# Writing a weight slab's low part over the raw slab, and loading the slot again after its last use

## The reference

```python
# first_block
proj = rmsnorm(x, g) @ w_in                       # 7 column groups per head, and two gates
o_a  = gated_delta_rule_chunked(q, k, v, g, beta) # 8 heads
o_b  = forgetting_attention(fq, fk, fv, log_f)    # 8 heads
merged = sigmoid(gate_a) * (o_a @ w_proj_gdn) + sigmoid(gate_b) * (o_b @ w_proj_fox)
h = x + merged @ w_out
x = h + square(relu(rmsnorm(h, g2) @ w_up)) @ w_down
# second_block
rq, rk, rv, rg, aq, ak, av, gate_a, gate_b = split(rms_norm(x, g) @ w_in_2 + b_in_2)
# retention on 4 heads, windowed attention on 16, each projected, gated and merged
x = x + merged @ w_out_2
x = x + (silu(h2 @ w_ffn_gate) * (h2 @ w_ffn_up)) @ w_ffn_down
return rms_norm(x, g3)
```

## Time and profile before

| | us |
|---|---|
| median of 3 executions (1887.64 to 1888.70) | 1888.69 |
| the profiled execution's own time | 1888.82 |
| its span, first to last instruction | 1887.0 |
| PE (matmul) busy | 1876.8, 99% of the span |
| GpSimd (POOL) busy | 1091.8, 58% |
| VectorE (DVE) busy | 1252.6, 66% |
| ScalarE (ACT) busy | 777.7, 41% |
| 16 DMA engines, slab queue | 27.9% of their time |

### The profile page before, as it was taken

How to read it: one execution, slowest core, us unless ns; L and a number is a source line. 1 busy time by engine, 2 the same in 40 slices (tenths; PEclk the granted TensorE clock), 3 DMA queues, 4 the chain that set the end, 5 groups by cost and what they waited for, 6 DMA issues and landing times.

```text
span 1887.0 us, 31991 instructions
## 1 busy us (share of the span) xinstructions
PE 1876.8 (99%) x11773; PEld 1606.0 (85%) x11773; DVE 1252.6 (66%) x2128; ACT 777.7 (41%) x1526; POOL 1091.8 (58%) x1221
## 2 busy tenths in 40 slices
PE   9999999999999999999999999999999999999998
PEld 7788888888888888899989888888888889999997
DVE  7877777767642248767775467787722368888882
ACT  5344433444342245333433544655432344333333
POOL 5454345543445477767776845445555585666665
PEclk9999999999999999999999999999999999999999
DMA  4212221221223332332334422122233323323232
GB/s 163 89 55 89 78 66 36 87 89 67 68 82 108 133 96 84 112 101 90 110 102 126 139 97 77 57 67 79 79 134 100 101 90 101 110 93 113 92 110 78
DMA packets 53470, 176.78 MB, mean 94 GB/s; under 512 B 7744, under 2 KB 8576, under 8 KB 53120
## 3 DMA queue, kind: packets, MB, share of 16 engines
q1 hardware_dynamic: 52880, 172.85, 27.9%
q10 hardware_dynamic: 496, 2.65, 0.5%
HBM read 171.26 MB, written 4.23 MB: 93 GB/s over the span
## 4 chain that ended last, share of the span: by engine, by line
PE 96%; DVE 2%; ACT 0%; DMA 0%; issue 0%; DVEq 0%; ACTq 0%
PE bank L322 17%; PE bank L324 17%; PE bank L323 17%; PE bank L862 6%; PE bank L864 6%; PE bank L863 6%; PE bank L912 5%; PE bank L913 5%; PE bank L914 5%; PE bank L2076 2%; PE bank L2070 2%; PE bank L2327 1%; PE bank L2087 1%; PE bank L2314 1%; PE bank L1276 1%; PE bank L1293 1%
## 5 line engine op out<-in xcount | busy, mean ns | idle before, releaser
L311 POOL TENSOR_TENSOR slab_lo<-slab_raw,slab_hi 128x256 fp32r<-128x256 f32 x1138 | 998.5, 913 | 741.7 <-ACT slab_hi L304 741.5
L322 PE MATMUL bank<-u_hi,slab_hi 128*128 128x512 f32 x1032 | 432.5, 419 | 0.1
L324 PE MATMUL bank<-u_hi,slab_lo 128*128 128x512 f32 x1032 | 404.1, 392 | 0.0
L323 PE MATMUL bank<-u_lo,slab_hi 128*128 128x512 f32 x1032 | 403.0, 390 | 0.0
L304 ACT CAST slab_hi<-slab_raw 128x1024 fp32r<-128x1024 f32 (+1 forms) x302 | 298.0, 997 | 97.4 <-PE bank L324 49.8
L324 PEld LDWEIGHTS bank<-u_hi,slab_lo 128*128 128x128 f32 x1032 | 193.7, 188 | 42.5
L322 PEld LDWEIGHTS bank<-u_hi,slab_hi 128*128 128x128 f32 x1032 | 194.3, 188 | 39.6 <-issue 4.1
L323 PEld LDWEIGHTS bank<-u_lo,slab_hi 128*128 128x128 f32 x1032 | 194.6, 189 | 35.4 <-issue 1.9
L912 PE MATMUL bank<-part_hi,slab_hi 128*128 128x512 f32 x384 | 149.8, 390 | 0.2 <-DVE residual L1034 0.2
L913 PE MATMUL bank<-part_lo,slab_hi 128*128 128x512 f32 x384 | 149.8, 390 | 0.0
L914 PE MATMUL bank<-part_hi,slab_lo 128*128 128x512 f32 x384 | 149.4, 389 | 0.0
(11 more groups left out here) (444 smaller groups left out, 4022.5 us busy)
## 6 DMA issues: line engine op xcount, KB each, us to landing
slab_raw<-slabs SPq DMA_DIRECT2D x302, 512.0 KB, 3.7
g_and_cum_rows<-row_store SPq DMA_DIRECT2D x7, 512.0 KB, 6.4
residual<-x_t SPq DMA_DIRECT2D x4, 512.0 KB, 6.2
residual<-x_t SPq DMA_DIRECT2D x1, 2048.0 KB, 9.1
residual_store<-residual SPq DMA_DIRECT2D x1, 2048.0 KB, 9.2
residual<-residual_store ACTq DMA_DIRECT2D x1, 2048.0 KB, 9.2
out_t<-result_tok SPq DMA_DIRECT2D x4, 256.0 KB, 2.3
out_t<-residual SPq DMA_DIRECT2D x4, 256.0 KB, 2.8
```

The lines of the kernel that those rows point to most:

```text
L311: ins = pool.tensor_tensor(w_lo[s][:, ks, :], raw[s][:, ks, :], w_hi[s][:, ks, :].bitcast(F32), ALU.subtract)
L322: pe.matmul(bank, w_hi[s][:, k, :], x_hi[:, k, :], start=first, stop=False)
L323: pe.matmul(bank, w_hi[s][:, k, :], x_lo[:, k, :], start=False, stop=False)
L324: mm = pe.matmul(bank, w_lo[s][:, k, :], x_hi[:, k, :], start=False, stop=last)
```

## The change

A second name, `raw_lo`, is put on the raw buffers, with the type of a low part. In all phases but the two feed-forward blocks POOL writes the low part there, over the raw slab that it reads (and DVE does for slab 0, L2516), and PE reads it there. Raw is then in use until PE is done with the slab, so SP's load into a slot waits for `s_used` where it waited for `s_lo`. This holds for the first four loads of each feed-forward block too, as their slots' slabs before are of the other kind. All other loads of the feed-forward blocks wait as before. `slab_lo` stays where it is; no buffer is moved, added or given up, and no instruction is added or taken away.

```diff
+        raw_lo = [at(f"slab_raw_lo{s}", [P, KT, P], s * 4 * KiB, F32R) for s in range(SLOTS)]
...
+        def in_place(ph, j):
+
+            if j >= ph.n and ph.iters == 1:
+                ph = phases[phases.index(ph) + 1]
+            return ph is not ph_mlp and ph is not ph_ffn
+
+        def low_of(ph, j):
+
+            return (raw_lo if in_place(ph, j) else w_lo)[ph.slot(j)]
+
         def load_slab(sp, ph, i, j):
-            wait_slab(sp, s_lo, ph, i, j)
+            wait_slab(sp, s_used if in_place(ph, j) or j < SLOTS else s_lo, ph, i, j)
...
-                ins = pool.tensor_tensor(w_lo[s][:, ks, :], raw[s][:, ks, :], w_hi[s][:, ks, :].bitcast(F32),
+                ins = pool.tensor_tensor(low_of(ph, j)[:, ks, :], raw[s][:, ks, :], w_hi[s][:, ks, :].bitcast(F32),
...
-                mm = pe.matmul(bank, w_lo[s][:, k, :], x_hi[:, k, :], start=False, stop=last)
+                mm = pe.matmul(bank, low_of(ph, j)[:, k, :], x_hi[:, k, :], start=False, stop=last)
...
-                sp.wait_ge(s_lo, j - SLOTS + 1)
+                sp.wait_ge(s_used, j - SLOTS + 1)
                 sp.dma_start(raw[s][:].rearrange("p k c -> p (k c)"), dram["slabs"][j, :, :]).then_inc(s_raw[s], 16)
...
-                        mm = pe.matmul(bank[:], w_lo[0][:, k, :], u_hi[:, k, :], start=False, stop=False)
+                        mm = pe.matmul(bank[:], raw_lo[0][:, k, :], u_hi[:, k, :], start=False, stop=False)
...
-                        mm = pe.matmul(bank[:], w_lo[j][:, k, :], u_hi[:, k, :], start=False, stop=k == KT - 1)
+                        mm = pe.matmul(bank[:], raw_lo[j][:, k, :], u_hi[:, k, :], start=False, stop=k == KT - 1)
...
-                    dve.tensor_tensor(w_lo[0][:], raw[0][:], w_hi[0][:].bitcast(F32), ALU.subtract).then_inc(s_lo, 1)
+                    dve.tensor_tensor(raw_lo[0][:], raw[0][:], w_hi[0][:].bitcast(F32), ALU.subtract).then_inc(s_lo, 1)
```

## The result

| | before | after |
|---|---|---|
| median of the runs | 1888.41 us (4 runs, 1887.64 to 1888.70) | 1933.28 us (4 runs, 1928.94 to 1937.97) |
| profiled execution | 1888.82 us, span 1887.0 | 1935.77 us, span 1934.0 |
| mean granted clock | 0.999 | 0.993 |

The ratio is 1.0235, 95% interval 1.0223 to 1.0248: 44.9 us slower. The forecast was 1912.8 us in 1903 to 1924. The sign was right; the time lies 9 us above the range.

The account below looks back on a forecast made before the run. PE, at work in 99% of the span, was taken as the bound. Seven head boundaries (21.7), round 0 to 1 (1.1) and the retention entry (1.2) sum to 24.0 us on 1888.82: 1912.8 us, range 1903 to 1924.

Parts of the forecast that it names:

- The two steps at the head boundaries: Seven head boundaries: late slabs 4 and 5 delay POOL's ors and rsc, so PE waits 1.8 and 1.3 us, 3.1 each.
- Step 1: Head boundary, slab 4: high part, low part and the ors behind it 1.9 us later; PE waits 1.8 us.
- Step 2: Head boundary, slab 5: high part, low part and rsc 3.7 us later; PE waits 1.3 us more.
- The aside that step 3's low part would come nearer 3.7 us: Head boundary, slab 6: POOL's low part contends with more DVE work, 0.4 us a boundary more.
- The aside on the transfer: Slab loads by the skill's fit take 3.2 us: each of seven boundaries 0.4 us less, the sum 2.8 less.
- The boundaries' sum: Seven head boundaries, rounds 1 to 2 up to 7 to the gate round: 7 x 3.1 = 21.7 us.
- step 3: Head boundary, slab 6: POOL's small step behind the low part comes 0.6 us late, within slack; costs nothing.
- the third entry also counts: Rival, 0.13: at head boundaries a longer transfer and low part pass slab 6's slack by 1.4 us; 10 more, 1922.6.
- Slots are reused after 4 slabs in the merges, the output projections and most of the retention part.: Three slabs, 16.4 us, lie between release and use against 8.4 needed, so these parts cost nothing.
- every microsecond for which PE is made to wait is added to the span: Whole kernel: PE works in 99% of the span, so PE's new waits count at their length.
- the entry to the retention part: From the ten slabs to the retention rounds, slot reused after 2: PE waits 1.2 us, ends 0.6 and 1.7.
- Round 0 to 1: ACT's store and reload of gate rows, behind slab 4's later high part: 1.1 us, ends 0 and 2.0.

Follow-up runs that it names:

- Experiment 3: Changed kernel with POOL's three fox steps (osq, cola, bm) put ahead of the low part at the same place of its queue: 1912.52 us, 1.0126.
- experiment 1: Changed kernel's load waits kept, but the low part written into its own tile as before the change: 1934.82 us, 1.0239.
- experiment 9: Changed kernel with exact waits in the retention rounds and POOL's osq and cola ahead of their low parts, bm behind its own: 1908.72 us, 1.0107.
- experiment 2: Changed kernel with SP's retention-round loads written out, so later rounds wait for the slab four back instead of two: 1921.65 us, 1.0168.
- Experiment 5: Changed kernel with eight extra PE products, result overwritten, while PE would wait for rsc at each head boundary: 1926.52 us, 1.0199.
- experiment 7: Kernel before with the change made in the head rounds and the gate round alone: 1916.17 us, 1.0149.

## Why the prediction was wrong

**Right: where and how.** The two steps at the head boundaries hold as predicted: high parts later by 1.9 and 3.9 us (1.9 and 3.7), `rsc` later by 3.9 (3.7), PE behind by 3.2 on average (3.1). Experiment 3 shows that the place in POOL's queue is the cause, experiment 1 that it is the wait alone. Step 1 was too large (PE waited 0.8 to 1.0 us instead of 1.8), because I carried over the low part's 3.71 us; with DVE idle beside most of it (367.86 to 370.21) it took 2.83. Step 2 took up what step 1 left (1.8 to 2.1 instead of 1.3), since `rsc` has its own time of arrival. So the sum came out (22.2 against 21.7 over all seven), as it hangs on step 2, though its parts were off by 0.5 to 1.0 us each. The aside that step 3's low part would come nearer 3.7 us did not hold: it took 2.80. The aside on the transfer, which rests on the Trainium skill (DMA: Bandwidth & Descriptors), did not show either. The boundaries' sum is 0.5 us above the forecast and not 2.8 below it, and the page gives its fit for transfers that GpSimd issues, where the slab loads are issued by SP.

**Right for a reason not named: step 3.** "Nothing" for `bm` held in the changed kernel, and experiment 9 shows why: the shift of the first two steps covers it. With them mended it costs 1.4 us a round. That is the number of the rival "the third entry also counts", but by chance: the rival had a longer transfer and a longer low part for it. I had named the cover for the present sum, not what comes due once the other two are gone.

**Wrong: "Slots are reused after 4 slabs in the merges, the output projections and most of the retention part."** This is true of the slots and false of the waits. The code takes the smallest distance that any round of a loop needs, and the first retention round's entry, two back, is imposed on the second and third:

```python
...
        if self.iters > 1 or wrap:
            dist.append(self.n + j0 - max(x for x in range(self.n) if x % SLOTS == s))
        if not wrap and self.last0[s] is not None:
            dist.append(self.first + j0 - self.last0[s])
        return min(dist) if dist else None
```

Before the change this wait, for a low part two back, cost nothing: the second round's load of slab 0 had landed at 1158.41, and ACT came to it at 1163.56. The change turned it into a wait for PE two back. It cost 12.6 us by the trace and 11 to 13 by experiment 2.

**Wrong: "every microsecond for which PE is made to wait is added to the span".** The sum had no term beyond the waits' length. Behind them the granted clock fell to half, which cost 7.9 us at the boundaries and some 4.5 (inside the 12.6) in the retention part of the profiled execution. Experiment 5 gives back 6.8 us by filling the first of these. The trace of before could not show it, as PE never stood still for long there; a bound above the waits' length would have been right.

**Too small: the entry to the retention part,** 2.6 instead of 1.2 us (ends 0.6 and 1.7). PE's first wait, 1.4, is what I worked out; behind it ACT, held by the same slab, is late with `ret_v_tok` and PE waits 1.0 more. I followed POOL's queue there and not ACT's. Round 0 to 1 was right (1.1, 1.0).

So of the 23.0 us missed in the profiled execution (20.5 in the median), 12.6 are the retention rounds, 7.9 the clock at the boundaries, 1.4 the entry, 0.7 the rest and 0.4 the boundaries and round 0 to 1 together.

## What to carry to other kernels

A wait is a semaphore and a number: before moving it to a later event, read the number that the code forms for every load, above all where one loop shares a single distance between its first round and the others. Small steps that the bounding engine wants at once should stand ahead of the bulk work that shares their place in an in-order queue, and after each such step is mended the next one has to be priced again. Where PE bounds a kernel, price a new idle time at its length and, as an upper end, at what the clock may lose behind it: here between nothing and 1.6 us a boundary.

## What the runs showed of the hardware

- Waits of PE of 0.8 to 1.0 and 1.8 to 2.1 us, 8 to 9 us apart, were followed at five of seven boundaries by 3.41 us at granted clock 0.50; with the second filled by eight products (experiment 5), at none in its profiled execution, and the mean clocks of all its five runs are alike (0.996 to 0.997). Waits of 1.4 us (the longest 1.5) once a round (experiment 9) were followed by none in the profiled execution, whose mean clock is 1.000; its other three runs have 0.998 to 0.999 and are 1.5 to 3.1 us longer, so a fall there is not excluded. In the retention part 3.8 us of waiting were followed by 6.83 and by 3.41 us. Whether a boundary had it or not differed between kernels with nearly the same waits (five in experiment 2, two in experiment 7); what decides was not tried.
- Runs of one kernel differ by the same thing: the four of the changed kernel span 9.0 us, with mean clocks of 0.995, 0.995, 0.993 and 0.991 from the shortest to the longest. The five of experiment 5 span 0.5 us. The four of experiment 1, with the changed kernel's waits, span 3.5, so kernels with the same waits need not spread alike.
- DVE's product of 40 columns took 0.20 us with POOL idle and 0.47 beside a low part of POOL, that of 56 columns 0.22 and 0.45, that of 24 columns 0.18 and 0.67. In one chain that PE waits for, holding the low part back gave 4.8 us in all, 0.67 us a round. The Trainium skill (GPSIMD Engine Reference, Key points) says that the two engines share SBUF interfaces and contend when DVE's instruction has two inputs in SBUF; these rows agree. In the other direction the same low part of a boundary took 3.71 us with two such steps of DVE beside it (L2626 at 347.07 and 348.15 in the trace before) and 2.83 with DVE idle from 367.86 to 370.21 (trace after).
